# Second feed-forward: the down product as two plain chunks and 28 steps of seven block products

## The reference, cut to what matters

```python
# second_block, DEPTH = 1, D_FF_2 = 4096
h2 = rms_norm_2(x, norm2[l])
x = x + jnp.square(jax.nn.relu(h2 @ w_up[l])) @ w_down[l]   # [1024,4096] @ [4096,1024]
return rms_norm_2(x, final_norm)

def rms_norm_2(x, g):
    y = x32 * lax.rsqrt(jnp.mean(x32 * x32, axis=-1, keepdims=True) + EPS)
    return y * g
```

## Time and profile before

| | us |
|---|---|
| time, median of 3 runs | 3029.94 (3027.96 to 3032.77) |
| the profiled execution: its span, for which no separate time is given | 3028.7 |
| PE busy in the span | 2909.7 (96%) |
| DVE busy | 1822.3 (60%) |
| ACT busy | 1191.0 (39%) |
| POOL busy | 538.9 (18%) |
| start of the down product's stage (end of the last pair but one) to the end of the span | 2637.7 to 3028.7 |

### The profile page before, as it was taken

One profiled execution on the slowest core, in us unless ns is written; L12 is line 12 of the kernel. 1 busy time (PEld: TensorE's weight loads), 2 busy tenths in 40 slices (PEclk: granted clock), 3 DMA queues, 4 the chain that ended last, 5 costly groups with the idle time before them and its releaser, 6 DMA issues.

```text
span 3028.7 us, 47692 instructions
## 1 busy us (share of the span) xinstructions
PE 2909.7 (96%) x20002; PEld 2338.6 (77%) x20002; DVE 1822.3 (60%) x2306; ACT 1191.0 (39%) x1769; POOL 538.9 (18%) x228
## 2 busy tenths in 40 slices
PE   8999988889899999999899999999899999999999
PEld 6877777777688888888688767666688888878887
DVE  3156778741799889444885455555456655554445
ACT  4155545632645555321543343444334333221112
POOL 3310122221100000444141200000021000043342
PEclk9999999999999999999999999999899999999999
DMA  6433430002422222322444634444544333342322
GB/s 210 152 114 112 126 114 25 27 32 78 159 70 84 84 84 77 133 111 84 132 149 147 208 105 126 147 135 136 195 132 132 105 112 111 125 160 84 112 84 111
DMA packets 252247, 350.09 MB, mean 116 GB/s; under 512 B 11377, under 2 KB 187642, under 8 KB 252034
## 3 DMA queue, kind: packets, MB, share of 16 engines
q1 hardware_dynamic: 237058, 299.85, 31.0%
q10 hardware_dynamic: 14976, 47.19, 4.1%
HBM read 238.17 MB, written 108.82 MB: 115 GB/s over the span
## 4 chain that ended last, share of the span: by engine, by line
PE 87%; DVE 5%; issue 3%; DMA 2%; ACT 2%; SPq 1%; POOL 0%; DVEq 0%; ACTq 0%
PE ps L480 36%; PE ps L3159 17%; PE ps L2929 10%; PE ps L2095 5%; PE ps L664 4%; PE ps L1512 4%; PE ps L2146 2%; PE ps L2165 2%; PE ps L2123 1%; PE ps L1575 1%; PE ps L2126 1%; DMA kl<-qk_lo 1%; PE ps L1553 0%; PE ps L506 0%; PE ps L2131 0%
## 5 line engine op out<-in xcount | busy, mean ns | idle before, releaser
L446 POOL TENSOR_TENSOR wl<-wraw,wh 128x1024 fp32r<-128x1024 f32 x62 | 157.2, 2537 | 1118.0 <-ACT wh L441 1108.4
L2734 DVE SCALAR_TENSOR_TENSOR y<-ps,token_s,y 128x1024 f32<-128x1024 f32 x120 | 154.0, 1284 | 164.1 <-PE ps L480 164.0
L480 PE MATMUL ps<-xh,wh 128*128 128x512 f32 x752 | 237.9, 398 | 5.4 <-DVE yb L1318 1.4
L480 PE MATMUL ps<-xl,wh 128*128 128x512 f32 x752 | 233.7, 392 | 0.0
L480 PE MATMUL ps<-xh,wl 128*128 128x512 f32 x752 | 233.2, 391 | 0.0
L441 ACT ACTIVATE wh<-wraw 128x1024 fp32r<-128x1024 f32 x78 | 82.4, 1058 | 268.1 <-PE ps L480 206.4
L480 PEld LDWEIGHTS ps<-xh,wh 128*128 128x128 f32 x752 | 139.8, 190 | 47.2 <-issue 9.4
L2996 DVE TENSOR_TENSOR y<-ps,y 128x1024 f32<-128x1024 f32 x79 | 96.8, 1225 | 125.6 <-PE ps L480 125.6
L2795 POOL TENSOR_TENSOR d2l<-d2raw,d2h 128x2048 fp32r<-128x2048 f32 x16 | 74.0, 4624 | 520.8 <-ACT d2h L2786 520.8
L480 PEld LDWEIGHTS ps<-xl,wh 128*128 128x128 f32 x752 | 142.4, 189 | 30.3
L480 PEld LDWEIGHTS ps<-xh,wl 128*128 128x128 f32 x752 | 142.3, 189 | 30.2
(11 more groups left out here) (487 smaller groups left out, 7477.3 us busy)
## 6 DMA issues: line engine op xcount, KB each, us to landing
wraw<-in_w_in SPq DMA_DIRECT2D x48, 512.0 KB, 4.9
r_raw<-in_w_up SPq DMA_DIRECT2D x38, 512.0 KB, 3.8
residual<-src ACTq DMA_DIRECT2D x32, 512.0 KB, 5.0
w_raw<-in_w_up SPq DMA_DIRECT2D x32, 512.0 KB, 5.1
act_d<-act SPq DMA_DIRECT2D x32, 512.0 KB, 6.2
d2raw<-in_w_down SPq DMA_DIRECT2D x16, 1024.0 KB, 5.0
f2raw<-act_d SPq DMA_DIRECT2D x16, 1024.0 KB, 7.1
proj<-stage SPq DMA_DIRECT2D x30, 512.0 KB, 3.1
```

The costliest lines, as they stand in the source:

```text
L446: nc.gpsimd.tensor_tensor(wl[:, s, :, :], wraw[:, s, :, :], wh[:, s, :, :].bitcast(F32), ALU.subtract).then_inc(w_lo, 1)
L480: mm = nc.tensor.matmul(ps[:, bank + h, :], w, x[:, h * HALF:(h + 1) * HALF], start=start and k == 0, stop=stop and k == 2)
L2734: ins = nc.vector.scalar_tensor_tensor(out=y[:, m, :], in0=bank2(2 + m % 2), scalar=token_s2[:, m:m + 1], in1=y[:, m, :], op0=ALU.mult, op ...
```

## The change

The down product's chunks 2 to 15 become 28 steps. A step g = 4c + m takes four feature tiles (pairs 2+2c and 3+2c) and the token tiles m and m+4, and makes the 256 tokens by 1024 columns from seven products of six matmuls. Before, the same work was eight blocks of six.

- **Operands.** The second operand's seven blocks (`b7_*`, from the weights) serve four steps: four 512 KB loads, four sums on DVE (`b7_sum`), fourteen roundings on ACT, seven remainders of 128 x 1024, four on DVE and three on POOL (`b7_rest`). The first operand's blocks (`a7_*`) are new for each step: two loads of 448 KB in pieces of 512 bytes, four roundings, and one remainder of 128 x 1792 on POOL. Its block sums are made in the up product's stage by POOL (`pair_act_sums`, four 128 x 512 a pair, for pairs 2 to 15) and stored as seven blocks in `act7_d`.
- **Sums.** ACT copies four of the seven PSUM results to SBUF, DVE adds seven parts of 128 x 512 to `y`: four from those copies, three from PSUM.
- **y unscaled.** `y` is kept without `token_s2`; the square's scale and the last scaling bring it in. The residual is divided by it instead (`token_inv`).
- **Residual.** In steps 0 to 7 PE turns one tile behind P2, ACT copies it out, SP stores it to `res_rows`; there is one buffer `rt`. In steps 10 to 17 the token rows are loaded and added on DVE (`add_rows`).
- **Chunks 0 and 1** stay plain, in the tile order 0, 1, 3, 4, 5, 6, 7, 2. Chunk 0 is copied to `y` by ACT (`token_copy`), chunk 1 added by DVE. `split_token_hi(0)` no longer waits for the store of pair 14, and `split_token_hi(1)` stands ahead of the copies.
- **The end.** `token_root_act` and `token_out` follow the last steps, two token tiles a step.

```diff
+        def a7_load(sp, g):
...
+            elif g >= 3:
+                s7_pe.wait(sp, "P4", g - 3)
+            if g >= 2:
+                a7_act.wait(sp, "h6", g - 2)
+            for k in range(2):
+                p = PLAIN2 + 2 * c + k
...
+                sp.dma_start(a7_raw[g % 3][:, :, k, :],
+                             act7_d[p, :, :, m * P:(m + 1) * P].rearrange("b p n -> p b n")).then_inc(f2_loaded[g % 2], 16)
+        def a7_rest(pool, g):
+            a7_act.wait(pool, "h6", g)
+            a7_pool.done(nc.gpsimd.tensor_tensor(a7_lo[g % 3][:, :, :, :], a7_raw[g % 3][:, :, :, :],
+                                                 a7_hi[g % 3][:, :, :, :].bitcast(F32), ALU.subtract), "lo")
+        def s7_products(pe, g):
+            c, m = divmod(g, 4)
+            s, u = c % 2, g % 3
+            a7_pool.wait(pe, "lo", g)
+            if g == 1:
+                pe.wait_ge(down_added, PLAIN_DONE)
+            for b, name in enumerate(PRODUCTS):
+                bank = s7_bank(g, PRODUCT_BANK[b])
+                if m == 0:
+                    if b < 4:
+                        b7_dve.wait(pe, f"l{b}", c)
+                    else:
+                        b7_pool.wait(pe, f"l{b}", c)
+                if name in ("P1", "P2", "P5") and g >= 2:
+                    s7_dve.wait(pe, {"P1": "y7", "P2": "y2", "P5": "y6"}[name], g - 2)
+                if name in ("P6", "P7", "P3", "P4"):
+                    s7_act.wait(pe, {"P6": "m1", "P7": "u2", "P3": "m5", "P4": "u3"}[name], g)
+                for i in range(2):
+                    a_hi, a_lo = a7_hi[u][:, b, i, :], a7_lo[u][:, b, i, :]
+                    b_hi, b_lo = b7_hi[s][:, b, i, :], b7_lo[s][:, b, i, :]
+                    for k, (w, x) in enumerate(((a_hi, b_hi), (a_hi, b_lo), (a_lo, b_hi))):
+                        mm = nc.tensor.matmul(ps[:, bank, :], w, x, start=PRODUCT_OPENS[b] and i == 0 and k == 0,
+                                              stop=i == 1 and k == 2, skip_group_check=True)
+                s7_pe.done(mm, name)
+                if name == "P2" and g < KT:
+                    turn_residual(pe, g)
+        def s7_copies(act, g, what):
+            name, bank, reader = {"m1": ("P1", 0, "y1"), "u2": ("P6", 0, "y3"), "m5": ("P5", 2, "y4"),
+                                  "u3": ("P7", 0, "y5")}[what]
+            s7_pe.wait(act, name, g)
+            s7_dve.wait(act, reader, g - 1)
+            s7_act.done(nc.scalar.activation(s7_part[what][:, :], ps[:, s7_bank(g, bank), :], ACT.Copy), what)
+        def s7_add(dve, g, what):
...
+            if of in s7_part:
+                s7_act.wait(dve, of, g)
+                part = s7_part[of][:, :]
+            else:
+                s7_pe.wait(dve, {1: "P2", 2: "P3", 0: "P4"}[of], g)
+                part = ps[:, s7_bank(g, of), :]
...
+            s7_dve.done(nc.vector.tensor_tensor(to, part, to, ALU.add), what)
+        def rt_load(sp, kt):
...
+                sp.wait_ge(rt_turned, kt)
+            sp.dma_start(rt[:, :], residual[kt]).then_inc(h_loaded[kt % 2], 16)
...
         def turn_residual(pe, kt):
-            pe.wait_ge(h_loaded[kt % 2], 16 * 16)
-            if kt >= 2:
-                pe.wait_ge(rt_added, kt - 1)
+            pe.wait_ge(h_loaded[kt % 2], 16 * (12 + kt // 2 + 1))
+            if kt:
+                rt_copied.wait(pe, "copied", kt - 1)
...
@@ the lists of SP, POOL, ACT, PE and DVE @@
+            for g in range(STEPS2):
+                if g + 2 < STEPS2:
+                    a7_load(sp, g + 2)
+                if g % 4 == 0 and g + 4 < STEPS2:
+                    b7_load(sp, g // 4 + 1)
+                if 1 <= g < KT:
+                    rt_load(sp, g)
+                if 1 <= g <= KT:
+                    store_residual(sp, g - 1)
+                if 0 <= g - ROWS_FIRST < TT:
+                    load_rows(sp, g - ROWS_FIRST)
...
-            for c in range(DOWN2):
-                split_token_lo(pool, c)
+            for g in range(STEPS2):
+                if g + 1 < STEPS2:
+                    a7_rest(pool, g + 1)
+                if g + 4 < STEPS2:
+                    for b in ((), (), (5,), (4, 6))[g % 4]:
+                        b7_rest(pool, b7_pool, g // 4 + 1, b)
...
-            for c in range(1, DOWN2):
-                split_token_hi(act, c)
-            token_roots_act(act, DOWN2 - 1)
+            split_token_hi(act, 1)
+            for k in range(TT):
+                token_copy(act, k)
+                if k >= 2:
+                    b7_round(act, 0, k - 2)
...
+                for what, count in (("m1", 3), ("u2", 1), ("m5", 1), ("u3", 9)):
+                    s7_copies(act, g, what)
+                    for rounds, *of in later[:count]:
+                        rounds(act, *of)
+                    del later[:count]
...
+            for g in range(STEPS2):
+                late = []
+                if g + 4 < STEPS2:
+                    c = g // 4 + 1
+                    if g % 4 == 1:
+                        late = [(b7_sum, c, name) for name in ("T1", "T2", "T4", "T3")]
+                    elif g % 4 >= 2:
+                        late = [(b7_rest, b7_dve, c, 2 * (g % 4) - 4 + k) for k in range(2)]
```

More of the change, by code:

```diff
@@ new lines, in b7_round, with b7_rest @@
+        def b7_round(act, c, k):
+            b, half = B7_ROUNDS[k // 2], k % 2
+            if b in (0, 1, 5):
+                b7_raw_ready(act, c)
+            else:
+                b7_dve.wait(act, {3: "T1", 2: "T2", 6: "T4", 4: "T3"}[b], c)
+            b7_act.done(nc.scalar.activation(b7_hi[c % 2][:, b, half, :], b7_raw[c % 2][:, b, half, :], ACT.Copy),
+                        f"h{b}{half}")
+        def b7_rest(eng, steps, c, b):
+            b7_act.wait(eng, f"h{b}1", c)
+            b7_dve.wait(eng, "T3", c)
+            op = nc.vector.tensor_tensor if b < 4 else nc.gpsimd.tensor_tensor
+            steps.done(op(b7_lo[c % 2][:, b, :, :], b7_raw[c % 2][:, b, :, :], b7_hi[c % 2][:, b, :, :].bitcast(F32),
+                          ALU.subtract), f"l{b}")
@@ L2713, in turn_residual @@
             mm.then_inc(rt_turned, 1)
[L2715 to L2736, removed]
@@ L2785, in split_token_hi @@
             act.wait_ge(d2_loaded[s], 16 * ((DOWN1 + 1 - s) // 2 + c // 2 + 1))
-            d2_act.done(nc.scalar.activation(d2h[s][:, :, :], d2raw[s][:, :, :], ACT.Copy), "dh")
+            for kt in range(2):
+                ins = nc.scalar.activation(d2h[s][kt][:, :], d2raw[s][:, kt, :], ACT.Copy)
+            d2_act.done(ins, "dh")
             act.wait_ge(f2_loaded[s], 16 * ((DOWN1 + 1 - s) // 2 + c // 2 + 1))
@@ L2964, in pair_squares @@
                 e7_dve.wait(dve, "c22", p)
-            e7_dve.done(nc.vector.scalar_tensor_tensor(out=act2[:, p % 2, row, :], in0=up[row][:, :], scalar=0.0,
-                                                       in1=up[row][:, :], op0=ALU.max, op1=ALU.mult), f"q{row}")
-        def store_pair(sp, p):
-            for row in range(2):
-                e7_dve.wait(sp, f"q{row}", p)
-                sp.dma_start(act2_d[2 * p + row], act2[:, p % 2, row, :]).then_inc(act2_stored[p % 2], 16)
+            tile = act2[:, p % 2, row, :]
@@ new lines, in pair_squares, with pair_act_sums @@
+            e7_dve.done(nc.vector.scalar_tensor_tensor(out=tile, in0=tile, scalar=0.0, in1=tile, op0=ALU.max,
+                                                       op1=ALU.mult), f"q{row}")
+        def pair_act_sums(pool, p):
+            j = p - PLAIN2
+            (a11, a21), (a12, a22) = ([act2[:, p % 2, row, h * HALF:(h + 1) * HALF] for h in range(2)] for row in range(2))
+            s2, s1 = (act_s21[:, h, :] for h in range(2))
+            tt = nc.gpsimd.tensor_tensor
+            e7_dve.wait(pool, "q1", p)
+            if j:
+                pool.wait_ge(sums_stored, 16 + 32 * j)
+            act_sums.done(tt(s1, a21, a22, ALU.add), "S1")
+            act_sums.wait(pool, "S1", j)
+            act_sums.done(tt(s2, s1, a11, ALU.subtract), "S2")
+            act_sums.done(tt(a21, a11, a21, ALU.subtract), "S3")
+            act_sums.wait(pool, "S2", j)
+            act_sums.done(tt(act_s4[:, :], a12, s2, ALU.subtract), "S4")
```

364 lines of the change are left out of this document (276 added, 88 removed).

## The result

| kernel | median us | runs | ratio to before (95%) | profiled span us |
|---|---|---|---|---|
| before, the same hour | 3030.30 | 4 | 1 | 3028.7 |
| after | 3101.46 (3099.98 to 3102.92) | 4 | 1.0236 (1.0221 to 1.0250) | 3101.2 |

The account below looks back on a forecast made before the run. The prediction took PE to bound the kernel, with 87% of the chain and only fewer matmuls helping in the down product; its terms summed to +65.5 us on the 3028.7 span, a time of 3095, range 3045 to 3120.

Parts of the forecast that it names:

- Products, transposes, last pair, up product, chunks: 168 fewer matmuls -38.1, cheaper transposes -1.3, ACT's wait gone -2.0, up product 0, chunk 0 +5.2, chunk 1 +2 us.
- term of 2 for chunk 1: In chunk 1 POOL's and DVE's queues for the steps' first operands compete: +2 us, bounds 0 and four times 2.4.
- Residual: Steps 1 to 7: PE waits for the residual tile's queued load, six times 4.2 us and once 9.5: +34.7 us.
- Clock: After seven waits of 4 us and more, matmuls run at the lower clock: +10 us, bounds 0 to 14.
- Steps 8 to 23: POOL and DVE take turns on work with two SBUF inputs, delaying PE: +45 us, between 0 and 68.
- much slower rival: PE's waits of 1 to 5 us in most steps keep the clock low: 1.4 us in 20 steps, 3123; chance 0.06.
- Steps 24 to 27: Sums end, but three steps carry two scalings and the last two weight remainders overhang: +8 us, bounds 0 and 15.
- End: Behind the last steps two token tiles are ready nearly together, so one more scaling and root: +2 us.
- Taking turns costs PE little: Rival on the steps: buffers hide POOL and DVE's turns; 3040 us, or 3065 with the lower bound's 25; chance 0.16.
- The residual is in time: Rival on steps 0 to 7: overlapping loads remove 34.7 and 10, but turns show there with 18; 3068 us, chance 0.12.
- faster rival: Rival on the steps: buffers absorb both turns and residual loads, so PE runs through; 2998 us, chance 0.06.

Follow-up runs that it names:

- e1: Against the changed kernel, SP issues each residual tile's load ahead of the loads of the step after next; 3059.01 us, ratio 1.0104 to before.
- e4: Against the changed kernel, POOL's remainders behind step 0 are cut short, PE multiplying rounded parts instead with as many matmuls; 3050.90 us, ratio 1.0081 to before.
- e6: The changed kernel with e1's edit, chunk 0's first two copies ahead of chunk 1's rounding, and POOL's remainders behind step 0 on DVE; 3005.85 us.

## Why the prediction was right

The direction, the three causes and their places were forecast; the size was 6 us short in the median. The account, from the up product's start, is +76.8 us (758.9 against 682.1) for a forecast of +65.5; 4.3 us went the other way ahead of it, in code that both kernels share.

- *Products, transposes, last pair, up product, chunks* (-38.1, -1.3, -2.0, 0, +5.2, +2). From the up product's start to the first product of chunk 2 before, of step 0 after, 366.2 us against 370.0: -3.8. In that stretch the forecast had -2.0, +5.2, +2 and the loss of 10.1 us of transposes that moved into the steps, -4.9. The up product has no wait but the 2.0 us that stood there before, ACT's is gone, and chunk 0 waits for 5.6. The term of 2 for chunk 1 was not seen by itself.
- *Residual* (+34.7, six times 4.2 and one of 9.5). Measured 36.6, seven times, the longest 10.0. Place in the queue and duration are both as worked out, and e1 shows that the place is the cause. The line rate of the Trainium skill (DMA: Bandwidth & Descriptors, Specifications) would have made it some 25 at the 435 GB/s that the prediction took, an estimate; at the some 358 GB/s that the same section gives as the limit of HBM per core, an estimate is some 32. The trace's 36.6 is above both; the rows' duration of such a load was right.
- *Clock* (+10, bounds 0 to 14). **This is the term that was mis-sized**: 15.7 in steps 0 to 7, and 14.6 without the 1.1 of drawing, still above my bound. I had taken it from one pair of waits of 2 us, which cost 1.4. Behind a wait of 4.5 us the transposes, too, are at the lower level; the 14.6 are 2.1 us for each of seven waits.
- *Steps 8 to 23* (+45). Measured 195.1 against 152.3 of products: 42.8. Groups of four took 45.2, 51.2, 50.7 and 48.0 us, in the forecast's 45 to 53. But I had thought of waits alone, and these are 30.3. PE is busy for 164.8 us, 12.5 more than its products want, and 2.3 more in steps 24 to 27. By the starts in PE's timeline 10.4 of these 14.8 are matmuls that followed each other more slowly, behind waits of up to 3 us: 6.9 of them in four stretches of starts 0.43 us apart, each behind a wait of 2.7 to 2.9 us, the rest in single late starts; what remains of the 14.8 is the last matmul before each of 27 waits. The much slower rival had named 28 for this. So that 42.8 lies this close to 45 is in part luck: the waits were smaller than forecast, and a loss that the term did not hold made up for it.
- *Steps 24 to 27* (+8). Measured 49.7 against 38.1, 11.6 in all: additions and copies still queue behind the last remainders and the scalings. *End* (+2): 10.5 us against 7.4, 3.1.

Added up, 5.7 of the 11.3 us that were missed are the clock's (1.1 of it drawing), 1.9 the residual's, 3.6 those of steps 24 to 27, and 2.2 were given back by steps 8 to 23; the chunks and the end have 1.1 each.

*The rivals.* "Taking turns costs PE little" falls: e4 gains 51.7 us from its absence. "The residual is in time" would have been e1, which is at 3059, not 3068: I had expected the turns to show in steps 0 to 7 with 18 us, and they show with 3.7 there and 3.3 later, perhaps because a step with transposes gives DVE and POOL a microsecond more, which no run shows. The faster rival's number was near: almost without waits the change gives 2992.94, and 2998 less chunk 0's 5.2 is 2992.8; so close a fit is chance, with 4.7 us of waits left.

The Trainium skill (GPSIMD Engine Reference, Key points) names exactly the condition, DVE instructions with two SBUF inputs; the runs agree, 0.684 us with a PSUM source and 1.46 to 1.61 without. The sentence gives no size, and the mild reading of it, a slowing of both, is what the timeline of step 11 speaks against: DVE's addition there ended 0.55 us behind POOL's instruction, with 3.96 us of its 4.51 spent beside it and still 0.55 us to go, most of the 0.69 that it takes alone.

## What to carry to other kernels

Before work is shared between POOL and DVE, add up the durations of the instructions on both that have two SBUF sources, as if they ran on one engine; if the sum exceeds the matmuls' time, move POOL's to DVE (which here needs 2.02 us for what takes POOL 4.07 at best), or let DVE read PSUM. Put a load that is needed soon ahead of the waits in its queue, not behind loads for later. And price a wait of PE with the time that the matmuls behind it lose at the lower clock: here 2.1 us, on average, for one of 4.1 to 10.0 us.

## What had not been expected

- Each of the seven waits for the residual, most of 4.1 to 4.7 us, cost PE another 2.1 us at the lower level; behind one of them eight transposes took 1.97 us for 1.03, and matmuls started 0.43 us apart. In steps 8 to 27 matmuls started late by 10.4 us in all behind the waits, which are 39.5 themselves.
- DVE had room for all of POOL's remainders: busy for 192.2 of 195.1 us in steps 8 to 23 before they were moved, for 158.8 of 164.4 after. A busy share counts the time in which an instruction stands still.
- What is left in e6, waits for a remainder on a DVE that has 158.8 us of work, was not tried further. Its row additions, 1.28 us each in steps 10 to 17, are the work there that could lie elsewhere.
